# Mixer gates, branches and their sum laid out by tokens instead of by columns, in an encoder kernel on one Trainium2 core

## The chip, the cores and the metric

The kernel runs on one core of one Trainium2 chip. The metric is the device time of one execution in microseconds (us). Before the change it is 1127.99 us, the median of three runs (1127.98 to 1128.56).

## What is computed

Input x is 256 tokens by 1024 channels, in float32. There are two layers; each is a token mixer followed by a feed-forward part (dense in layer 0, eight experts in layer 1). The change is in the mixer, which runs twice:

```python
proj = rms_norm(x) @ w_in + b_in              # 1024 x 6144: q, k, v, u_f, u_x, u_g, gates
y_a = neighbourhood_attention(q, k, v, rpb)   # 8 heads of 64
y_b = fourier_mix(u_f)
y_c = recurrent_branch(u_x, u_g, ...)         # conv, two scans, GeLU gate
y_br = einsum('bskc,kcd->bskd', stack(y_a, y_b, y_c), w_branch)   # 3 x (512 -> 1024)
g = sigmoid(gates).reshape(b, s, 3, 1024)
merged = sum(g * y_br, axis=2)
x = x + merged @ w_out
```

The sigmoid is computed as (1 + tanh(z / 2)) / 2, the factor 1/2 being applied when the sum is split.

## The kernel before

**Weights and units.** All large products run as units. One unit is 512 KB of weights: SyncE loads it into a ring (`raw`, six places), ScalarE rounds it into `w_hi` (L514), VectorE takes the rest into `w_lo` (L900), and TensorE multiplies high by high, high by low and low by high (`mm3`, L1441 to 1445). Rings of four places for `w_hi` and `w_lo` let the splits run three units ahead of TensorE: ScalarE's loop for unit k ends with the high half of unit k+3, which waits until TensorE has done unit k-1; VectorE's loop does likewise.

**A mixer** has 68 units. Units 0 to 47 are twelve groups of four: a group is 512 output columns of `w_in` and 256 rows of it a unit. Their order is u_f, u_x, q, k, v, u_g, and then the six gate groups (units 24 to 47). Units 48 to 59 are the branches, two a product; for each half of the output channels the branches come as Fourier, recurrent, attention. Units 60 to 67 are `w_out`. A group collects in PSUM banks 0 and 1 or 2 and 3, by turns.

**Two orientations.** `unit_columns` (L1452) has the weights stationary and the activations moving: 24 matmuls a unit of 128x256, output with channels on partitions. `unit_tokens` (L1467) has the activations stationary and the weights moving: 12 matmuls a unit of 128x512, output with tokens on partitions. Before, only u_f and v use the second; `w_out` uses its wide relative (L1498).

**Between the units** TensorE does the small products in an order written out by hand: Fourier at units 8 and 12, the recurrent gates at 16 and 25 (L1611), attention at every other unit from 28 (scores L1627, values L1639, transposes L1650). ScalarE and VectorE go through a hand-written list by unit number too. Of the backward scan: at unit 22 ScalarE takes a square root (L676), at 23 VectorE multiplies (L1142), at 24 VectorE takes the second half of u_g (L1042) and runs the forward scan (L1149), and at 25 ScalarE's tanh (L650) waits for that scan and for TensorE's products. These belong to the forward scan up to L1149 and to the backward scan from L650 on.

**Gates, branches, sum.** The gates' bias is one column a channel tile: ScalarE empties a gate group by four tanh of 128x256 with a bias column (L629). A branch product is multiplied by 1 + gate on VectorE (L1182); after the third, two pairs of additions (L1190, L1195) give the sum, ScalarE and VectorE split it straight into `xh` and `xl` (L707, L1202), channels on partitions, as `w_out` needs it.

**GpSimd's queue.** `row` is one tile of 1024 columns in which a vector stands on all 128 partitions; `load_row` (L459) fills it by a DMA. In a mixer it holds the bias of v and u_f, and after VectorE has emptied v (L1029) the next norm's scale is loaded into it.

Of the kernel before, what the change touches and what calls it, by code (L numbers as in the profile page):

```python
# [8 lines left out]
F32 = mybir.dt.float32  # L9
# [8 lines left out]
P = 128  # L18
# [88 lines left out]
def build(nc, x, norm_mix_g, w_in, b_in, rpb, conv_w, conv_b, lru_wa, lru_ba, lru_wx, lru_bx,  # L107
# [12 lines left out]
    with ExitStack() as ctx:  # L120
# [3 lines left out]
        def sem(name):  # L124
# [13 lines left out]
        gates = sb("gates", [P, 3 * KC, SEQ])  # L138
        gflat = gates[:, :, :].rearrange("p c s -> p (c s)")
        hn = gflat[:, 0:TT * D].rearrange("p (t d) -> p t d", t=TT)  # L140
        junk = gflat[:, TT * D:2 * TT * D].rearrange("p (t d) -> p t d", t=TT)
# [55 lines left out]

        O_SP, O_NSP, O_HBA, O_HBX, O_BQ, O_GB = 0, 16, 32, 48, 64, 72
        lam_w = small[:, 96:192].rearrange("p (a b) -> p a b", a=6)
# [50 lines left out]
            sem("s_ps"), sem("s_max"), sem("p_exp"), sem("p_norm"), sem("pt_ps"), sem("pt_ok"), sem("av_ps"), sem("ya_h"), sem("ya_l"))  # L250
        merged, mh_ok, ml_ok = sem("merged"), sem("mh_ok"), sem("ml_ok")

# [16 lines left out]
        ACT_EVACS = [g not in (UF, V) for g in GROUPS] + [False] * len(BRANCHES)  # L269
        DVE_EVACS = [g < GATE0 for g in GROUPS] + [True] * len(BRANCHES)  # L270

        def group_end(l, n):
# [185 lines left out]
        def _(pool):  # L458
# [15 lines left out]
            def mixer(l):  # L474
                load_row(b_in, l * IN_COLS + 2 * BR, normed, 2 * TT * (2 * l + 1))
                for hp in range(HEADS // 2):
                    mask_tables(l, hp)
                load_row(norm_ffn_g, l * D, evac_d, evacs(DVE_EVACS, l, GROUPS.index(V)))

# [18 lines left out]
        def _(act):  # L498
# [69 lines left out]
            def enter(n, B):  # L568
# [10 lines left out]
                for b in range(2):  # L579
                    norm_hi(n, 1, b)  # L580

            def mixer(l):
                B = BASE_MIX[l]
# [16 lines left out]
                for k in range(U_MIX):  # L600
# [9 lines left out]
                    if k <= U_IN and k % 4 == 0 and n >= 0 and ACT_EVACS[n]:  # L610
                        g = GROUPS[n]
                        act.wait_ge(unit_used, group_end(l, n))
                        b0 = 2 * (n % 2)
                        bc = l * NB + 4 * g
                        if g == Q:
                            for m in range(2):
                                i = act.activation(q_t[:, m, :], ps[:, b0, SEQ * m:SEQ * m + SEQ], ACT.Identity,
                                                   scale=SCALE, bias=col2[:, O_BQ + 4 * l + m:O_BQ + 4 * l + m + 1])
                        elif g in (K, UX, UG):
                            for m in range(2):  # L620
                                dst = {K: k_t[:, m, :], UX: ux_t[:, m, 2:2 + SEQ],
                                       UG: ug_t[:, SEQ * m:SEQ * m + SEQ]}[g]
                                i = act.activation(dst, ps[:, b0, SEQ * m:SEQ * m + SEQ], ACT.Identity,
                                                   bias=col[:, bc + m:bc + m + 1])
                        else:

                            for m in range(4):
                                gb = col2[:, O_GB + 24 * l + 4 * (g - GATE0) + m:O_GB + 24 * l + 4 * (g - GATE0) + m + 1]
                                i = act.activation(gates[:, 4 * (g - GATE0) + m, :],  # L629
                                                   ps[:, b0 + m // 2, SEQ * (m % 2):SEQ * (m % 2) + SEQ],  # L630
                                                   ACT.Tanh, scale=0.5, bias=gb)
# [70 lines left out]
                    for dg in range(2):  # L702
                        if k == U_IN + 6 * (dg + 1) + 1:
                            for b in range(2):
                                act.wait_ge(merged, 4 * l + 2 * dg + b + 1)
                                at = 1024 * dg + 512 * b
                                act.activation(xhf[:, at:at + 512], gflat[:, at:at + 512],  # L707
                                               ACT.Copy, scale=0.5).then_inc(mh_ok, 1)
# [177 lines left out]
        def _(dve):  # L886
# [15 lines left out]
            def norm(n, t):  # L902
                dve.wait_ge(rms_ok, TT * n + t + 1)
                link(dve.reciprocal(rinv[:, t:t + 1], rms[:, t:t + 1]))
                if t == 0 and n:
                    dve.wait_ge(row_in, 16 * {1: 2, 2: 3, 3: 5, 4: 6}[n])
                for half in range(2):
# [56 lines left out]
            def set_up_columns():  # L964
# [6 lines left out]
                for l in range(2):  # L971
                    dve.tensor_scalar(col2[:, O_BQ + 4 * l:O_BQ + 4 * l + 4], col[:, l * NB + 4 * Q:l * NB + 4 * Q + 4],
                                      SCALE, None, ALU.mult)
                    dve.tensor_scalar(col2[:, O_GB + 24 * l:O_GB + 24 * l + 24],
                                      col[:, l * NB + 4 * GATE0:l * NB + 4 * GATE0 + 24], 0.5, None, ALU.mult)
                dve.tensor_scalar(lam_w[:, 5, :], col[:, O_LAM:O_LAM + 16], -1.0, 0.0, ALU.mult, ALU.max).then_inc(col_ok, 1)
# [20 lines left out]
            def mixer(l):  # L997
# [15 lines left out]
                for k in range(U_MIX):  # L1013
# [5 lines left out]
                    if k <= U_IN and k % 4 == 0 and n >= 0 and DVE_EVACS[n]:  # L1019
# [4 lines left out]
                        if g in (UF, V):  # L1024
                            dve.wait_ge(row_in, 16 * (3 * l + 1))
                            for t in range(TT):
# [148 lines left out]
                    if U_IN < k <= U_IN + U_BR and (k - U_IN) % 2 == 0:  # L1175
# [3 lines left out]
                        dve.wait_ge(evac_a, evacs(ACT_EVACS, l, n))  # L1179
                        for b in range(2):  # L1180
                            at = br * 2048 + 1024 * dg + 512 * b
                            i = dve.scalar_tensor_tensor(out=gflat[:, at:at + 512], in0=gflat[:, at:at + 512],  # L1182
                                                         scalar=1.0, in1=ps[:, 2 * (n % 2) + b, :],
                                                         op0=ALU.add, op1=ALU.mult)
                        i.then_inc(evac_d, 1)
                        if nb % 3 == 2:
                            dve.wait_ge(evac_d, evacs(DVE_EVACS, l, n))
                            for b in range(2):
                                at = 1024 * dg + 512 * b
                                i = dve.tensor_tensor(gflat[:, 2048 + at:2048 + at + 512], gflat[:, 2048 + at:2048 + at + 512],  # L1190
                                                      gflat[:, 4096 + at:4096 + at + 512], ALU.add)
                            link(i)
                            for b in range(2):
                                at = 1024 * dg + 512 * b
                                dve.tensor_tensor(gflat[:, at:at + 512], gflat[:, at:at + 512],  # L1195
                                                  gflat[:, 2048 + at:2048 + at + 512], ALU.add).then_inc(merged, 1)
                    for dg in range(2):
                        if k == U_IN + 6 * (dg + 1) + 1:
                            for b in range(2):
                                dve.wait_ge(mh_ok, 4 * l + 2 * dg + b + 1)  # L1200
                                at = 1024 * dg + 512 * b
                                dve.scalar_tensor_tensor(out=xlf[:, at:at + 512], in0=gflat[:, at:at + 512], scalar=0.5,  # L1202
                                                         in1=xhf[:, at:at + 512].bitcast(F32), op0=ALU.mult,
                                                         op1=ALU.subtract).then_inc(ml_ok, 1)
# [233 lines left out]
        def _(pe):  # L1438
# [27 lines left out]

            def unit_tokens(base, k, r, banks, i=0, per=0):  # L1467

                wh, wl = split(base, k, i, per)
                for kk in range(2):  # L1470
                    for t in range(TT):
                        c = 2 * r + kk
                        ins = mm3(ps[:, banks + t, :], xh[:, c, P * t:P * t + P], xl[:, c, P * t:P * t + P],
                                  wh[:, 512 * kk:512 * kk + 512], wl[:, 512 * kk:512 * kk + 512],
                                  first=(c == 0), last=(c == KC - 1))
                ins.then_inc(unit_used, 1)

            def unit_tokens_tile(base, k, r, bank, t):
# [74 lines left out]
            def mixer(l):  # L1553
# [11 lines left out]
                for k in range(4, U_MIX - 4):  # L1565
# [86 lines left out]
                    if k < U_IN:  # L1652
# [6 lines left out]
                        if GROUPS[n] in (UF, V):  # L1659
                            unit_tokens(B, k, r, 2 * (n % 2))  # L1660
                        else:
                            unit_columns(B, k, r, 2 * (n % 2), (xhf, xlf), SEQ, last=KC - 1)
                    elif k < U_IN + U_BR:
# [10 lines left out]
                        unit_columns(B, k, r, 2 * (n % 2), (yhf[:, 1024 * br:1024 * br + 1024], ylf[:, 1024 * br:1024 * br + 1024]),  # L1674
                                     SEQ, last=BC - 1)
# [261 lines left out]
```

## Time and profile before

| what | value |
|---|---|
| median of three runs | 1127.99 us |
| profiled execution | 1127.95 us |
| its span, first to last instruction | 1126.1 us |
| mean granted TensorE clock | 0.992 |
| TensorE busy | 1105.6 us (98%) |
| VectorE busy | 871.0 us (77%) |
| ScalarE busy | 720.6 us (64%) |
| mixer of layer 0, first unit to last | about 10 to 234 us |
| mixer of layer 1 | about 440 to 664 us |

The busy times are sums over the whole span. The records of neighbouring matmuls overlap, so the time that a matmul takes from the next one is the distance between their starts, not its length.

### The profile page before, as it was taken

To read this page: it belongs to the slowest core of one execution; us is meant where nothing else is said; L and a number is where in the kernel's file an instruction comes from. 1 tells how busy PE (TensorE), PEld (TensorE's weight loads), DVE (VectorE), ACT (ScalarE), POOL (GpSimd) and SP (SyncE) were. 2 spreads that over 40 slices of the span, in tenths; PEclk is the share of its full clock that TensorE was granted. 3 is DMA by queue.
4 is the path that set the end of the run, shared out by engine and by line. 5 is a ranking of instruction groups with operands and counts; after the bars stand their busy time and mean duration, and the time that the engine had idled before them with its cause. 6 is when DMAs were issued, how large, how long until landed. Compare 5 with 4: busy or idle time off the path is not lost.

```text
span 1126.1 us, 19254 instructions
## 1 busy us (share of the span) xinstructions
PE 1105.6 (98%) x6858; PEld 970.8 (86%) x6858; DVE 871.0 (77%) x1064; ACT 720.6 (64%) x978; POOL 53.7 (5%) x29
## 2 busy tenths in 40 slices
PE   7999999999999999999999999999999999999996
PEld 6989999989999998989989988878888888888884
DVE  6975885864554457766885868999999999999996
ACT  6376664464444446356665457888888888887884
POOL 0300000000000000200000000101010101101010
PEclk9999999999999999999999998999999999999998
DMA  9955445565555657755445469999999999999951
GB/s 307 248 167 156 141 146 186 179 194 184 186 174 161 222 186 211 207 160 176 134 140 182 159 229 399 371 379 347 362 362 354 382 336 391 339 389 334 389 210 40
DMA packets 139500, 276.47 MB, mean 246 GB/s; under 512 B 26608, under 2 KB 26928, under 8 KB 139440
## 3 DMA queue, kind: packets, MB, share of 16 engines
q1 hardware_dynamic: 136976, 267.20, 70.1%
q0 software_dynamic: 2304, 8.39, 2.0%
q8 instruction: 39, 0.64, 0.2%
q14 instruction: 21, 0.17, 0.0%
q10 hardware_dynamic: 160, 0.07, 0.0%
HBM read 273.52 MB, written 2.10 MB: 245 GB/s over the span
## 4 chain that ended last, share of the span: by engine, by line
PE 88%; DVE 6%; ACT 4%; issue 1%; DMA 0%; DVEq 0%; ACTq 0%
PE ps L1443 27%; PE ps L1445 27%; PE ps L1444 27%; PE ps L1611 1%; DVE w_lo L900 1%; ACT w_hi L514 1%; PE ps L1764 1%; PE ps L1835 1%; PE ps L1639 1%; DVE yl L900 1%; PE ps L1585 1%; ACT p_t L695 1%; PE ps L1750 1%; PE ps L1650 1%; PE ps L1529 1%
## 5 line engine op out<-in xcount | busy, mean ns | idle before, releaser
L900 DVE TENSOR_TENSOR w_lo<-raw,w_hi 128x1024 fp32r<-128x1024 f32 x268 | 326.1, 1233 | 154.3 <-ACT w_hi L514 152.1
L514 ACT ACTIVATE w_hi<-raw 128x1024 fp32r<-128x1024 f32 x268 | 281.4, 1059 | 180.3 <-PE ps L1445 177.6
L1443 PE MATMUL ps<-xh,w_hi 128*128 128x256 f32 x960 | 274.5, 286 | 0.0
L1444 PE MATMUL ps<-xl,w_hi 128*128 128x256 f32 x960 | 271.6, 283 | 0.0
L1445 PE MATMUL ps<-xh,w_lo 128*128 128x256 f32 x960 | 271.6, 283 | 0.0
L1443 PEld LDWEIGHTS ps<-xh,w_hi 128*128 128x128 f32 x960 | 184.1, 192 | 2.6 <-issue 2.1
L1444 PEld LDWEIGHTS ps<-xl,w_hi 128*128 128x128 f32 x960 | 184.1, 192 | 0.4
L1445 PEld LDWEIGHTS ps<-xh,w_lo 128*128 128x128 f32 x960 | 184.0, 192 | 0.0
L1443 PE MATMUL ps<-w_hi,xh 128*128 128x512 f32 x432 | 172.0, 398 | 1.1 <-DVE xl L927 0.8
L1444 PE MATMUL ps<-w_lo,xh 128*128 128x512 f32 x432 | 169.2, 392 | 0.0
L1445 PE MATMUL ps<-w_hi,xl 128*128 128x512 f32 x432 | 169.1, 392 | 0.0
L900 DVE TENSOR_TENSOR w_lo<-mix,w_hi 128x1024 fp32r<-128x1024 f32 x128 | 152.6, 1219 | 11.0 <-ACT w_hi L514 8.7
L514 ACT ACTIVATE w_hi<-mix 128x1024 fp32r<-128x1024 f32 x128 | 134.4, 1060 | 32.8 <-PE ps L1445 32.7
L1443 PEld LDWEIGHTS ps<-w_hi,xh 128*128 128x128 f32 x432 | 81.8, 189 | 22.3 <-DVE w_lo L900 2.6
L1445 PEld LDWEIGHTS ps<-w_hi,xl 128*128 128x128 f32 x432 | 81.7, 189 | 17.5
L1444 PEld LDWEIGHTS ps<-w_lo,xh 128*128 128x128 f32 x432 | 81.7, 189 | 16.1
L900 DVE TENSOR_TENSOR yl<-mix,yh 128x1024 fp32r<-128x1024 f32 x64 | 77.1, 1218 | 0.7
L514 ACT ACTIVATE yh<-mix 128x1024 fp32r<-128x1024 f32 x64 | 67.8, 1062 | 15.2 <-PE ps L1445 15.2
L1443 PE MATMUL ps<-w_hi,yh 128*128 128x512 f32 x192 | 76.6, 399 | 0.7
L1445 PE MATMUL ps<-w_hi,yl 128*128 128x512 f32 x192 | 75.0, 390 | 0.0
L1444 PE MATMUL ps<-w_lo,yh 128*128 128x512 f32 x192 | 74.9, 390 | 0.0
L1443 PE MATMUL ps<-yh,w_hi 128*128 128x256 f32 x192 | 54.5, 284 | 0.0
(229 smaller groups left out, 1591.1 us busy)
## 6 DMA issues: line engine op xcount, KB each, us to landing
mix<-in_moe_w_gu_dram SPq DMA_DIRECT2D x112, 512.0 KB, 7.6
raw<-in_w_in_dram SPq DMA_DIRECT2D x96, 512.0 KB, 4.3
raw<-in_moe_w_gu_dram SPq DMA_DIRECT2D x80, 512.0 KB, 5.8
mix<-in_moe_w_down_dram SPq DMA_DIRECT2D x80, 512.0 KB, 5.5
raw<-in_ffn_w_gu_dram SPq DMA_DIRECT2D x48, 512.0 KB, 4.0
raw<-in_w_branch_dram SPq DMA_DIRECT2D x24, 512.0 KB, 3.6
raw<-in_ffn_w_down_dram SPq DMA_DIRECT2D x24, 512.0 KB, 4.7
raw<-in_w_out_dram SPq DMA_DIRECT2D x16, 512.0 KB, 3.5
```

Of the source, the lines that this page charges most:

```text
L514: act.activation(halves(u)[0], src, ACT.Copy).then_inc(hi_done, 1)
L695: ins = act.activation(p_t[:, j % 2, hh, :], p_t[:, j % 2, hh, :], ACT.Exp, bias=nmax[:, j % 2, hh:hh + 1], accum_out=rsum[:, j % 2, hh:hh ...
L900: dve.tensor_tensor(w_l, place(u)[0], w_h.bitcast(F32), ALU.subtract).then_inc(lo_done, 1)
L1443: mm(dst, ah, bh, start=first, stop=False, skip_group_check=True)
L1444: mm(dst, ah, bl, start=False, stop=False, skip_group_check=True)
L1445: return mm(dst, al, bh, start=False, stop=last, skip_group_check=True)
L1529: ins = pe.transpose(dst, hn[:, t, P * (4 * b + c):P * (4 * b + c) + P], ident)
L1585: ins = mm(ps[:, 4 + m, 0:SEQ], uf_t[:, BR * t + P * m:BR * t + P * m + P], cst[:, at:at + SEQ], start=(t == 0), stop=(t == TT - 1))
L1611: ins = mm(ps[q, 4 + 2 * g + m // 2, SEQ * (m % 2):SEQ * (m % 2) + SEQ], wlru[q, d, g, m, :], conv_t[q, m, :], start=True, stop=True)
L1639: ins = mm(ps[HD * hh:HD * hh + HD, 6, P * t:P * t + P], v_t[:, kt, HD * hd:HD * hd + HD], pt_t[:, hh, P * kt:P * kt + P], start=(kt == 0) ...
L1650: ins = pe.transpose(ps[:, 7, at:at + P], p_t[:, j % 2, hh, P * kt:P * kt + P], ident)
L1750: ins = pe.transpose(ps[:, 6 + c // 4, P * (c % 4):P * (c % 4) + P], xrow[:, P * c:P * c + P], ident)
```

## The change

Gate groups and branch products go from `unit_columns` to `unit_tokens`. The gate bias can then no longer be a column of ScalarE's tanh; it is copied as rows into the PSUM banks before the group (`seed`), and the group's first matmul adds to it. `row` gets three more loads a mixer. The sum comes out with tokens on partitions, and TensorE turns it by transposes (`turn_merged`).

```diff
+                for j in range(3):          # GpSimd, after v is emptied
+                    if j:
+                        load_row(b_in, l * IN_COLS + BR * GATE0 + D * j, seeded, 6 * l + 2 * j)
+                    else:
+                        load_row(b_in, l * IN_COLS + BR * GATE0, evac_d, evacs(DVE_EVACS, l, GROUPS.index(V)))
+                load_row(norm_ffn_g, l * D, seeded, 6 * l + 6)
...
+            def seed(l, j):                 # ScalarE
+                n = len(GROUPS) - 6 + j
+                act.wait_ge(row_in, 16 * (6 * l + 2 + j // 2))
+                act.wait_ge(evac_a, evacs(ACT_EVACS, l, n - 2))
+                act.wait_ge(evac_d, evacs(DVE_EVACS, l, n - 2))
+                for t in range(TT):
+                    ins = act.activation(ps[:, 2 * (n % 2) + t, :], row[:, BR * (j % 2):BR * (j % 2) + BR], ACT.Copy)
+                ins.then_inc(seeded, 1)
...
-                            for m in range(4):
-                                i = act.activation(gates[...], ps[:, b0 + m // 2, ...], ACT.Tanh, scale=0.5, bias=gb)
+                            for t in range(TT):
+                                i = act.activation(by_token[:, t, gate_columns(g)], ps[:, b0 + t, :], ACT.Tanh, scale=0.5)
+                    if 22 <= k < U_IN - 4 and k % 4 == 2:
+                        seed(l, (k - 22) // 4)
...
-                        if k == U_IN + 6 * (dg + 1) + 1:
+                        if k == U_IN + 6 * (dg + 1) + (3, 2)[dg]:     # ScalarE; VectorE alike
+                            for t in range(TT):
+                                act.wait_ge(mt_ps, TT * (2 * l + dg) + t + 1)
+                                act.activation(xh[...], ps[:, (4, 0)[dg] + t, :]..., ACT.Copy, scale=0.5)
...
+            def turn_merged(l, dg):         # TensorE
+                pe.wait_ge(merged, 2 * l + dg + 1)
+                for t in range(TT):
+                    for c in range(4):
+                        at = 512 * dg + P * c
+                        ins = pe.transpose(ps[:, (4, 0)[dg] + t, P * c:P * c + P], by_token[:, t, at:at + P], ident)
+                    ins.then_inc(mt_ps, 1)
...
+                        elif GROUPS[n] >= GATE0:
+                            if r == 0:
+                                pe.wait_ge(seeded, 6 * l + n - len(GROUPS) + 7)
+                            unit_tokens(B, k, r, 2 * (n % 2), seed=True)
...
+                        if k == U_IN + 8:
+                            turn_merged(l, 0)
+                        unit_tokens(B, k, r, 2 * (n % 2), ah=yh, al=yl, c0=BC * br, last=BC - 1)
...
-                        if r % 2 == 0:
-                            pe.wait_ge(ml_ok, 4 * l + r // 2 + 1)
+                        if r == 0:
+                            pe.wait_ge(ml_ok, 4 * l + 2)
+                        if r == 2:
+                            turn_merged(l, 1)
```

On VectorE the products and sums keep their number and size (128x512) and address token rows; the sum of the second and third branch's products is taken one branch earlier. The bias columns halved for the tanh are no longer set up. The waits that count `row` loads get the new numbers.

## Rows read from the trace of the kernel before

**Rows 1.** The page: busy time of the engines, and engines on the chain.

```profile
PE 1105.6 (98%) x6858; PEld 970.8 (86%) x6858; DVE 871.0 (77%) x1064; ACT 720.6 (64%) x978; POOL 53.7 (5%) x29
...
PE 88%; DVE 6%; ACT 4%; issue 1%; DMA 0%; DVEq 0%; ACTq 0%
```

**Rows 2.** The chain of waits around the attention of layer 0 (start, us, what).

```profile
104.96 0.66 PE ps L1627 x4
...
140.94 0.44 DVE yl L1120
...
141.51 0.51 PE ps L1639 x5
```

**Rows 3.** Busy time by stretch: first unit 28 to 38, then the branches.

```profile
104.90:141.50 36.60, 35.93 (x293) 32.88 (x293) 30.43 (x48) 26.60 (x53) 0.00 (x0) 1.00 0.45 136
177.40:212.50 35.10, 35.10 (x296) 34.93 (x296) 24.71 (x29) 15.60 (x19) 0.00 (x0) 1.00 0.55 179
```

**Rows 4.** Timeline of TensorE, units 16 to 20 (start, us, line, shape).

```profile
67.31 0.40 PE L1444 MATMUL ps<-w_lo,xh 128*128 128x512 f32 x1
...
77.76 0.39 PE L1445 MATMUL ps<-w_hi,xl 128*128 128x512 f32 x1
77.99 0.28 PE L1443 MATMUL ps<-xh,w_hi 128*128 128x256 f32 x1
...
80.86 0.28 PE L1443 MATMUL ps<-xh,w_hi 128*128 128x256 f32 x1
```

**Rows 5.** Timeline of TensorE, eight transposes between matmuls of the dense part.

```profile
264.57 1.04 PE L1694 MATMUL ps<-cst,gates 128*128 128x128 f32 x8
...
265.56 0.28 PE L1444 MATMUL ps<-xl,w_hi 128*128 128x256 f32 x1
```

**Rows 6.** Loads of the row tile: start in layer 0, issues with us to landing.

```profile
80.07 0.58 POOL L463 DMA_DIRECT2D row<-in_norm_ffn_g_dram  x1 [29.85 <-DVE mix L1029]
...
row<-in_norm_ffn_g_dram POOLq DMA_DIRECT2D x1, 512.0 KB, 6.6
...
row<-in_norm_ffn_g_dram POOLq DMA_DIRECT2D x1, 512.0 KB, 7.3
...
DMA to landing us min/median/max: 5.2/6.6/7.3
```

**Rows 7.** Timeline of ScalarE, units 22 to 25; idle time before in brackets.

```profile
82.20 1.28 ACT L676 ACT_TABLE_LOAD   x1
...
92.85 1.28 ACT L650 ACT_TABLE_LOAD   x1 [1.37 <-DVE mix L1149]
96.19 1.57 ACT L650 ACTIVATE mix<-ps,col 128x256 f32<-128x256 f32 x4 [2.05 <-PE ps L1611]
```

**Rows 8.** Timeline of VectorE, units 22 to 28.

```profile
85.53 1.22 DVE L900 TENSOR_TENSOR w_lo<-raw,w_hi 128x1024 fp32r<-128x1024 f32 x1 [1.10 <-ACT w_hi L514]
...
89.70 0.88 DVE L1042 TENSOR_SCALAR mix<-ps,col 128x256 f32<-128x256 f32 x2 [0.39 <-PE ps L1445]
90.49 2.28 DVE L1149 TENSOR_TENSOR_SCAN mix<-mix 128x1024 f32<-128x1024 f32 x1
...
105.64 0.69 DVE L1105 TENSOR_TENSOR p_t<-ps,mix 128x512 f32<-128x512 f32 x1 [0.38 <-PE ps L1627]
```

**Rows 9.** Timeline of ScalarE at unit 32: a gate group emptied, and a 128x512 copy.

```profile
121.74 1.57 ACT L629 ACTIVATE gates<-ps,col 128x256 f32<-128x256 f32 x4
123.18 0.61 ACT L690 ACTIVATE pt_t<-ps 128x512 f32<-128x512 f32 x1
123.66 0.53 ACT L695 ACTIVATE p_t<-p_t,small 128x256 f32<-128x256 f32 x1
```

**Rows 10.** Timelines of VectorE and TensorE at unit 42.

```profile
155.86 0.42 DVE L1120 TENSOR_TENSOR yl<-ps,yh 128x256 fp32r<-128x256 f32 x1 [0.71 <-ACT yh L701]
...
156.62 0.66 PE L1639 MATMUL ps<-pt_t,mix 128*64 128x128 f32 x8
```

**Rows 11.** Timeline of VectorE at unit 60: the last product, before the sum.

```profile
212.84 1.28 DVE L1182 SCALAR_TENSOR_TENSOR gates<-gates,ps 128x512 f32<-128x512 f32 x2 [0.50 <-PE ps L1445]
```

More of the change, by code:

```diff
@@ L139, in build @@
         gflat = gates[:, :, :].rearrange("p c s -> p (c s)")
+        by_token = gflat.rearrange("p (t n) -> p t n", t=TT)
         hn = gflat[:, 0:TT * D].rearrange("p (t d) -> p t d", t=TT)
@@ L196, in build @@
         N_COL = O_LAM + 4 * BC
-        O_SP, O_NSP, O_HBA, O_HBX, O_BQ, O_GB = 0, 16, 32, 48, 64, 72
+        O_SP, O_NSP, O_HBA, O_HBX, O_BQ = 0, 16, 32, 48, 64
         lam_w = small[:, 96:192].rearrange("p (a b) -> p a b", a=6)
@@ L250, in build @@
             sem("s_ps"), sem("s_max"), sem("p_exp"), sem("p_norm"), sem("pt_ps"), sem("pt_ok"), sem("av_ps"), sem("ya_h"), sem("ya_l"))
-        merged, mh_ok, ml_ok = sem("merged"), sem("mh_ok"), sem("ml_ok")
+        seeded, merged, mt_ps, mh_ok, ml_ok = sem("seeded"), sem("merged"), sem("mt_ps"), sem("mh_ok"), sem("ml_ok")
         ft_ps = sem("ft_ps")
@@ L270, in build, with gate_columns @@
         DVE_EVACS = [g < GATE0 for g in GROUPS] + [True] * len(BRANCHES)
+        def gate_columns(g):
+            return slice(512 * (g - GATE0), 512 * (g - GATE0) + 512)
         def group_end(l, n):
@@ L625, in mixer @@
                         else:
-                            for m in range(4):
[L628 to L631, printed above, removed]
+                            for t in range(TT):
+                                i = act.activation(by_token[:, t, gate_columns(g)], ps[:, b0 + t, :], ACT.Tanh, scale=0.5)
                         i.then_inc(evac_a, 1)
+                    if 22 <= k < U_IN - 4 and k % 4 == 2:
+                        seed(l, (k - 22) // 4)
                     if k == AT_F1:
@@ L702, in mixer @@
                     for dg in range(2):
-                        if k == U_IN + 6 * (dg + 1) + 1:
[L704 to L707, printed above, removed]
+                        if k == U_IN + 6 * (dg + 1) + (3, 2)[dg]:
+                            for t in range(TT):
+                                act.wait_ge(mt_ps, TT * (2 * l + dg) + t + 1)
+                                act.activation(xh[:, 4 * dg:4 * dg + 4, P * t:P * t + P],
+                                               ps[:, (4, 0)[dg] + t, :].rearrange("p (c s) -> p c s", c=4),
                                                ACT.Copy, scale=0.5).then_inc(mh_ok, 1)
@@ L905, in norm @@
                 if t == 0 and n:
-                    dve.wait_ge(row_in, 16 * {1: 2, 2: 3, 3: 5, 4: 6}[n])
+                    dve.wait_ge(row_in, 16 * {1: 5, 2: 6, 3: 11, 4: 12}[n])
                 for half in range(2):
@@ L1024, in mixer @@
                         if g in (UF, V):
-                            dve.wait_ge(row_in, 16 * (3 * l + 1))
+                            dve.wait_ge(row_in, 16 * (6 * l + 1))
                             for t in range(TT):
@@ L1179, in mixer @@
                         dve.wait_ge(evac_a, evacs(ACT_EVACS, l, n))
[L1180 to L1183, printed above, removed]
+                        a, b, c = (slice(D * i + 512 * dg, D * i + 512 * dg + 512) for i in range(3))
+                        q = (a, b, c)[br]
+                        for t in range(TT):
+                            i = dve.scalar_tensor_tensor(out=by_token[:, t, q], in0=by_token[:, t, q],
+                                                         scalar=1.0, in1=ps[:, 2 * (n % 2) + t, :],
                                                          op0=ALU.add, op1=ALU.mult)
@@ L1187, in mixer @@
                             dve.wait_ge(evac_d, evacs(DVE_EVACS, l, n))
[L1188 to L1191, printed above, removed]
+                            for t in range(TT):
+                                i = dve.tensor_tensor(by_token[:, t, a], by_token[:, t, a], by_token[:, t, b], ALU.add)
@@ L1192, in mixer @@
+                            i.then_inc(merged, 1)
+                        elif nb % 3 == 1:
+                            dve.wait_ge(evac_d, evacs(DVE_EVACS, l, n))
+                            for t in range(TT):
+                                i = dve.tensor_tensor(by_token[:, t, b], by_token[:, t, b], by_token[:, t, c], ALU.add)
                             link(i)
[L1193 to L1196, printed above, removed]
@@ L1197, in mixer @@
                     for dg in range(2):
[L1198 to L1203, printed above, removed]
+                        if k == U_IN + 6 * (dg + 1) + (3, 2)[dg]:
+                            for t in range(TT):
+                                at = (slice(None), slice(4 * dg, 4 * dg + 4), slice(P * t, P * t + P))
+                                dve.wait_ge(mh_ok, TT * (2 * l + dg) + t + 1)
+                                dve.scalar_tensor_tensor(out=xl[at], in0=ps[:, (4, 0)[dg] + t, :].rearrange("p (c s) -> p c s", c=4),
+                                                         scalar=0.5, in1=xh[at].bitcast(F32), op0=ALU.mult,
@@ L1465, in unit_columns, with unit_tokens @@
                 return ins
-            def unit_tokens(base, k, r, banks, i=0, per=0):
+            def unit_tokens(base, k, r, banks, i=0, per=0, ah=xh, al=xl, c0=0, last=KC - 1, seed=False):
                 wh, wl = split(base, k, i, per)
@@ L1472, in unit_tokens @@
                         c = 2 * r + kk
-                        ins = mm3(ps[:, banks + t, :], xh[:, c, P * t:P * t + P], xl[:, c, P * t:P * t + P],
+                        ins = mm3(ps[:, banks + t, :], ah[:, c0 + c, P * t:P * t + P], al[:, c0 + c, P * t:P * t + P],
                                   wh[:, 512 * kk:512 * kk + 512], wl[:, 512 * kk:512 * kk + 512],
-                                  first=(c == 0), last=(c == KC - 1))
+                                  first=(c == 0 and not seed), last=(c == last))
                 ins.then_inc(unit_used, 1)
+            def turn_merged(l, dg):
+                pe.wait_ge(merged, 2 * l + dg + 1)
+                for t in range(TT):
+                    for c in range(4):
+                        at = 512 * dg + P * c
+                        ins = pe.transpose(ps[:, (4, 0)[dg] + t, P * c:P * c + P], by_token[:, t, at:at + P], ident)
+                    ins.then_inc(mt_ps, 1)
             def unit_tokens_tile(base, k, r, bank, t):
@@ L1673, in mixer @@
                                 pe.wait_ge(y_ok, count)
-                        unit_columns(B, k, r, 2 * (n % 2), (yhf[:, 1024 * br:1024 * br + 1024], ylf[:, 1024 * br:1024 * br + 1024]),
-                                     SEQ, last=BC - 1)
+                        if k == U_IN + 8:
+                            turn_merged(l, 0)
+                        unit_tokens(B, k, r, 2 * (n % 2), ah=yh, al=yl, c0=BC * br, last=BC - 1)
                     else:
                         r = k - U_IN - U_BR
-                        if r % 2 == 0:
-                            pe.wait_ge(ml_ok, 4 * l + r // 2 + 1)
+                        if r == 0:
+                            pe.wait_ge(ml_ok, 4 * l + 2)
+                        if r == 2:
+                            turn_merged(l, 1)
                         unit_wide(B, k, xh[:, r, :], xl[:, r, :], TT, r == 0, False)
```

3 lines of the change are left out of this document (removed).

## The prediction, made before the changed kernel was run

> **What bounds the kernel now.** I read the page first: TensorE is busy 98% of the span and holds 88% of the chain that ended last [rows 1]. That says TensorE, but the chain has a second part. Asked in order of time, it leaves TensorE at 104.96 us, at unit 28 where attention begins, and comes back only at 141.51 at unit 38; between the two it runs through ScalarE and VectorE alone [rows 2]. In the same stretch TensorE is busy 35.93 of 36.60 us [rows 3]: the two other engines deliver just in time, and TensorE waits once, about 0.7 us. Layer 1 has the same rows. So a mixer has three kinds of place: before unit 28 and after unit 42 a shorter TensorE unit is a shorter run, and in the branches TensorE is busy 35.10 of 35.10 us [rows 3]; between 28 and 42 it is the list of ScalarE and VectorE that counts, and TensorE saves nothing there.
>
> **A unit on TensorE.** Starts, not lengths, give the price. From 67.31 to 77.76 us there are 46 steps of 128x512: 10.45 / 46 = 0.227 us. From 77.99 to 80.86 there are 24 steps of 128x256: 0.120 us [rows 4]. A unit by columns is 24 x 0.120 = 2.88 us, one by tokens 12 x 0.227 = 2.73 us: 0.153 us less (with 0.12 and 0.19 as ends, by the rounding of the starts). 36 units a mixer change: 24 of gates, 12 of branches.
>
> **Turning the sum.** It is new: eight transposes twice a mixer. In the dense part eight of them stand between matmuls: from the first of them to the second matmul behind them 0.99 us, less one step of 0.12, is 0.87 us [rows 5]. Four turns cost 3.5 us (upper end 4.2, by their recorded 1.04 us). Their waits should be free: at unit 60 VectorE starts the product 0.5 us into its turn, two of it take 1.28 us [rows 11], and the one pair of additions left behind it I take as long; 2.6 us, against 5.4 us until TensorE turns at unit 62. After that the copy and the split of two 128x512 tiles, about 2 us, have two units again before the second half of `w_out`. The turn at unit 56 has the same 5.4 us, and its split three units. If one such cover were gone, a turn would show at most some 2 us more.
>
> **ScalarE's list.** Emptying a gate group is four tanh of 128x256, started 1.44 us apart from what follows (121.74 to 123.18); a 128x512 instruction goes in 0.48 us (123.18 to 123.66) [rows 9]. So the tanh become 0.96, a gain of 0.48, and the seed adds two copies, 0.96 us. A copy from `row` into PSUM is not in the trace: between 0.36 (the 128x256 step) and 0.61 us (the recorded length); I take 0.48, the nearest in shape. Six times a mixer ScalarE has 0.48 us more. Seeds 2 to 5 (units 30, 34, 38, 42) fall where it waits for VectorE several us anyway. They delay only things that have slack.
>
> **The first seed, which decides.** It stands at unit 22, ahead of the square root, in a queue that runs in order. Its bias row is asked for when v is emptied: in the trace GpSimd issues the load of the same tile at the same place at 80.07 us, and it takes 6.6 us to land in layer 0 and 7.3 in layer 1, where the shortest load of this tile took 5.2 [rows 6]. Nothing before unit 20 changes, so I take these two numbers. ScalarE reaches the seed at about 82.20 [rows 7] and stands until 86.67; the two copies end at 87.65. Behind it wait the square root, the high halves of units 25 and 26, and the first half of u_g. TensorE does not yet suffer: it has its units up to 24, and the small products at 25 give it 3.6 us. VectorE does. Its low half of unit 25 comes 5.4 us late, then the product, the low half of 26, u_g and the forward scan run without the 0.4 us pause that they have now [rows 8]. ScalarE's table load and tanh at unit 25 wait for that scan. Now the load comes at 92.85 and ScalarE then waits 2.05 us for TensorE before the tanh [rows 7]. The delay is thus 5.4 - 0.4 - 2.0 = 3.0 us in layer 0 and 3.7 in layer 1. In general it is the landing time less 3.6 us; below 3.6 us it is nothing.
>
> From there it goes 1:1 into the attention. The second seed (unit 26) adds 0.96 us; VectorE's pause of 0.38 before the first scores' sum is used up [rows 8], which makes 3.6; the tanh at unit 32, which are on the chain [rows 2, 9], give back 0.48. So the list is 3.1 us late at unit 38 (layer 0) and 3.8 (layer 1). TensorE, which would be 0.6 us early at unit 28, catches up with the list and waits there by bits, at units 32, 34, 36 and 38, for VectorE's maxima and the split of the attention output. The last such place is unit 42: the split at 155.86 takes 0.42 us, TensorE starts 0.15 us behind such a split, hence at 156.43 + 3.1 = 159.5 in place of 156.62 [rows 10]: +2.9, and +3.6 in layer 1.
>
> **The sum.** From unit 42 to 47 six units give back 0.9 us: +2.0 and +2.7. The branches give 24 x 0.153 = 3.7 us back over both layers, the turns take 3.5. Together 2.0 + 2.7 - 3.7 + 3.5 = +4.5 us. The profiled execution had 1127.95 us (span 1126.1), which is the median of the runs to 0.04; so 1132.4 us.
>
> The later row loads cost nothing: the second is asked for after seed 1, near 102 us, and needed at unit 30, near 115; the third after seed 3, with four units again. GpSimd waits in between with nothing else queued. TensorE's own wait for the first seed is covered: copied by 87.7, needed at 89.6.
>
> **A rule that speaks otherwise.** Rows 6 have 6.6 and 7.3 us. The Trainium skill, page DMA: Bandwidth & Descriptors, section Anatomy of one DMA, gives for transfers issued from GpSimd about 2.0 us plus bytes over 436 GB/s, an estimate of 3.2 us for these 512 KB. By it the row would be there before the 3.6 us from which the delay counts, and the time would be that of rival 1. The trace disagrees by twice, on this very queue and tile.
>
> **Rivals.**
> 1. *The first seed's wait hides* (faster): the row lands within 3.6 us of its issue, or ScalarE and VectorE take up the delay. For it: GpSimd's queue is idle before it, and ScalarE has pauses of 1 to 2 us at each unit there. Against it: rows 6, and that VectorE is nearly solid from unit 25 to 28's start. Then the list is 0.96 - 0.38 - 0.48 = +0.1 late, TensorE at unit 42 -0.1, at 48 -1.0 a mixer: -2.0 - 3.7 + 3.5 = -2.2: 1125.7 us. Chance 0.20.
> 2. *TensorE alone counts* (faster): all 72 units give 0.153 us, less the turns: -11.0 + 3.5 = -7.5: 1120.4 us. Rows 1 speak for it, rows 2 against. Chance 0.05.
> 3. *Half of the delay is absorbed* (no change): the load lands in its shortest time, 5.2 us, in both layers, so that the delay is 1.6 instead of 3.0 and 3.7: 4.5 - 3.5 = +1.0: 1129.0 us. Chance 0.15.
> 4. *A turn waits as well* (slower by more): with VectorE behind, the sum is late for unit 56 or 62, up to 2 us for each of four turns, beside +4.5: some 1136. Rows 11 leave 2.8 us for it. Chance 0.08.
>
> The forecast has 0.52. What is below 0.2% (2.3 us) this kernel's measurement can't tell from no change, so the bounds are 1125.7 and 1130.3. Slower: forecast 0.50, rival 4, a part of 3: 0.60. Same: most of 3, half of 1 (which lies on the bound): 0.22. Faster: 0.18. The range is 1125.3 to 1134.6: at the lower end rival 1, at the upper the forecast with landings a us longer in both layers; the forecast's own range is 1130 to 1134.
>
> **What the profile after would show.** Steps of 0.227 us in gate and branch units. ScalarE idle 4 to 5 us ahead of the first seed, ended by the DMA of `row`; the forward scan ending near 97.8 instead of 92.8 us; the first scores' sum on VectorE near 109 instead of 105.64; TensorE waiting at units 32 to 38 for VectorE; the values product of unit 42 near 159.5. No wait ahead of the transposes. I am wrong if the first seed does not wait, or if the scan's delay meets a pause on ScalarE or VectorE that I have counted as work.

## The result, and the profile after

| | before | after | predicted |
|---|---|---|---|
| median | 1127.99 us | 1135.42 us (5 runs, 1133.58 to 1137.5) | 1132.4 (1125.3 to 1134.6) |
| ratio | | 1.006, 95% interval 1.0049 to 1.0071 | 1.0039 |
| profiled execution, its span | 1127.95, 1126.1 | 1135.58, 1133.4 | |
| end of mixer 0 / mixer 1 (first turn of the norm) | 233.62 / 663.80 us | 236.73 / 669.68 us | +1.9 / +4.5 |
| from there to the end of the span | 462.3 us | 463.7 us | 0 |

The changed kernel is slower, as forecast and for the reason forecast, but by 7.4 us in place of 4.5, and the time lies 0.8 us above the range. Of the 7.3 us between the two spans, 3.1 arise in mixer 0, 2.8 in mixer 1 (all of it behind its unit 20, where the changed kernel is still 3.1 us late), and 1.4 behind both mixers, where the change has no instruction. The last term was not in the prediction. Another 0.3 us lies outside the span: the device time is 2.2 us longer than the span in the changed kernel and 1.9 us in the kernel before. The two medians are 1.0066 apart, in the upper part of the interval; beside the experiments below, the kernel before had medians of 1128.7 to 1128.9 us and the changed kernel once 1135.08, which is 6.4 us in place of 7.4.

First the page of the changed kernel, against [rows 1]. TensorE has less work (832 fewer matmul records) and holds 10 points less of the chain; what it lost went to VectorE, ScalarE, issue and DMA. An engine that was made cheaper and holds less of the chain points to a new wait.

```profile
PE 1102.6 (97%) x6026; PEld 927.6 (82%) x6026; DVE 868.0 (77%) x1062; ACT 725.6 (64%) x978; POOL 56.6 (5%) x35
...
PE 78%; DVE 8%; ACT 8%; issue 3%; DMA 2%; SPq 0%; DVEq 0%; ACTq 0%
```

The chain of waits around unit 22 of layer 0 (start, us, what) names it. Before, the chain was TensorE's until 104.96 [rows 2]; now it leaves at v's emptying and goes through the load of the bias row.

```profile
78.66 1.29 DVE mix L1045 x2
80.25 7.34 DMA row<-in_b_in_dram
88.75 1.28 ACT L694
...
91.01 1.05 ACT w_hi L524
...
93.37 1.24 DVE mix L1158
94.64 1.23 DVE w_lo L918
95.86 0.79 DVE mix L1058 x2
96.64 2.21 DVE mix L1165
98.92 1.28 ACT L668
```

ScalarE's timeline, against [rows 7] (start, us, line; idle time before in brackets): the seed stands 5.25 us for the row, and the table load at unit 25 then waits for the scan. The tanh starts at 100.22 instead of 96.19.

```profile
87.61 1.12 ACT L599 ACTIVATE ps<-row 128x512 f32<-128x512 f32 x2 [5.25 <-DMA row<-in_b_in_dram]
88.75 1.28 ACT L694 ACT_TABLE_LOAD   x1
...
98.92 1.28 ACT L668 ACT_TABLE_LOAD   x1 [4.26 <-DVE mix L1165]
100.22 1.57 ACT L668 ACTIVATE mix<-ps,col 128x256 f32<-128x256 f32 x4
```

VectorE's timeline, against [rows 8]: it idles 7.48 us for ScalarE's high half of unit 25, the scan starts at 96.56 instead of 90.49, the first scores' sum at 110.25 instead of 105.64.

```profile
92.08 1.22 DVE L918 TENSOR_TENSOR w_lo<-raw,w_hi 128x1024 fp32r<-128x1024 f32 x1 [7.48 <-ACT w_hi L524]
...
96.56 2.28 DVE L1165 TENSOR_TENSOR_SCAN mix<-mix 128x1024 f32<-128x1024 f32 x1
...
110.25 0.68 DVE L1121 TENSOR_TENSOR p_t<-ps,mix 128x512 f32<-128x512 f32 x1
```

TensorE's timeline: it waits for VectorE at units 32, 34, 36, 38 and 42. The values product of unit 38 stands at 145.70 (141.51 in [rows 2]), that of 42 at 160.61 (156.62 in [rows 10]).

```profile
119.69 0.70 PE L1652 MATMUL ps<-mix 64*128 64x256 f32 x4 [1.34 <-DVE small L1124]
...
127.87 0.70 PE L1652 MATMUL ps<-mix 64*128 64x256 f32 x4 [0.93 <-DVE small L1124]
...
136.12 0.70 PE L1652 MATMUL ps<-mix 64*128 64x256 f32 x4 [0.88 <-DVE small L1124]
...
145.70 0.66 PE L1664 MATMUL ps<-pt_t,mix 128*64 128x128 f32 x8 [1.24 <-DVE yl L1136]
...
160.61 0.66 PE L1664 MATMUL ps<-pt_t,mix 128*64 128x128 f32 x8 [0.27 <-DVE yl L1136]
```

Busy time by stretch, against [rows 3]: TensorE is busy 35.42 of 40.80 us in the attention where it was 35.93 of 36.60, and still 35.10 of 35.10 in the branches.

```profile
104.90:145.70 40.80, 35.42 (x173) 25.86 (x173) 32.44 (x49) 31.21 (x58) 0.53 (x1) 1.00 0.51 167
180.50:215.60 35.10, 35.10 (x165) 28.98 (x165) 26.87 (x32) 15.41 (x18) 0.00 (x0) 1.00 0.54 179
```

### The profile page after: what moved, and what is told of

Its sections match the earlier page's. It is cut to its first block, busy times and chain, and to the rows that moved or that the text cites. A ratio compares the mean times of both kernels' runs of the same rounds, so it can differ in the third digit from the quotient of the medians.

```text
span 1133.4 us, 17620 instructions
## 1 busy us (share of the span) xinstructions
PE 1102.6 (97%) x6026; PEld 927.6 (82%) x6026; DVE 868.0 (77%) x1062; ACT 725.6 (64%) x978; POOL 56.6 (5%) x35
## 4 chain that ended last, share of the span: by engine, by line
PE 78%; DVE 8%; ACT 8%; issue 3%; DMA 2%; SPq 0%; DVEq 0%; ACTq 0%
PE ps L1459 24%; PE ps L1461 24%; PE ps L1460 24%; ACT w_hi L524 2%; DVE w_lo L918 2%; DMA row<-in_b_in_dram 1%; PE ps L1796 1%; PE ps L1867 1%; ACT mix L668 1%; ACT p_t L713 1%; DVE small L1123 1%; DVE p_t L1121 1%; ACT mix L678 1%; PE ps L1636 1%; DMA raw<-in_w_in_dram 1%
## 5 line engine op out<-in xcount | busy, mean ns | idle before, releaser
L1459 PE MATMUL ps<-w_hi,xh 128*128 128x512 f32 x624 | 249.8, 400 | 1.3 <-DVE xl L945 0.8
L1460 PE MATMUL ps<-w_lo,xh 128*128 128x512 f32 x624 | 244.3, 392 | 0.0
L1461 PE MATMUL ps<-w_hi,xl 128*128 128x512 f32 x624 | 244.3, 391 | 0.0
L1459 PE MATMUL ps<-xh,w_hi 128*128 128x256 f32 x576 | 164.0, 285 | 0.0
L1460 PE MATMUL ps<-xl,w_hi 128*128 128x256 f32 x576 | 163.0, 283 | 0.0
L1461 PE MATMUL ps<-xh,w_lo 128*128 128x256 f32 x576 | 162.9, 283 | 0.0
L1459 PEld LDWEIGHTS ps<-xh,w_hi 128*128 128x128 f32 x576 | 110.5, 192 | 0.5
L1460 PEld LDWEIGHTS ps<-xl,w_hi 128*128 128x128 f32 x576 | 110.5, 192 | 0.4
L1461 PEld LDWEIGHTS ps<-xh,w_lo 128*128 128x128 f32 x576 | 110.5, 192 | 0.0
L1459 PEld LDWEIGHTS ps<-w_hi,yh 128*128 128x128 f32 x288 | 54.1, 188 | 14.9 <-issue 3.9
```

What stands on the lines that cost most here:

```text
L1459: mm(dst, ah, bh, start=first, stop=False, skip_group_check=True)
L1460: mm(dst, ah, bl, start=False, stop=False, skip_group_check=True)
L1461: return mm(dst, al, bh, start=False, stop=last, skip_group_check=True)
```

## The experiments

Each comes with runs of the kernel before on the same chip; ratios are to those.

**Seed 0 moved to where ScalarE idles** (end of unit 23, behind the high half of unit 26), all else as changed.

```diff
-                    if 22 <= k < U_IN - 4 and k % 4 == 2:
+                    if 26 <= k < U_IN - 4 and k % 4 == 2:
                         seed(l, (k - 22) // 4)
...
+                    if k == 23:
+                        seed(l, 0)
```

> The changed kernel with the first seed alone moved, from the start of unit 22 on ScalarE's list to the end of unit 23. All loads, copies, units and turns stay. Theory (the first seed's wait for its row stands ahead of the square root and delays the list of ScalarE and VectorE by some 4 us a mixer): the wait is then after the high half of unit 26, near 88 us, when the row has just landed; the list is on time, TensorE is level at unit 42 and about 1 us ahead at unit 48, and the time is 1125 to 1127.5 us. Rival (the three added loads, or ScalarE's added copies, cost the time, wherever the first wait stands): 1133 us or more, since none of them is taken away. Rival (the matmuls by tokens or the turns are dearer than I counted): 1130 or more.

Measured 1127.88 us, ratio 0.9989 (0.998 to 0.9999), 0.4 us above the range of the theory. ScalarE's timeline:

```profile
88.14 1.10 ACT L599 ACTIVATE ps<-row 128x512 f32<-128x512 f32 x2
...
96.35 1.57 ACT L668 ACTIVATE mix<-ps,col 128x256 f32<-128x256 f32 x4 [1.92 <-PE ps L1638]
```

The seed starts half a microsecond later than in the changed kernel, yet nothing waits: the row is there, and ahead of the tanh 1.92 us of waiting for TensorE are back. So it is not the seed's work but what stands behind it in the queue while it waits. The first scores' sum is at 106.38, +0.74 to before (0.6 forecast for the second seed's copies), and mixer 1 ends at 661.92, 1.9 us earlier than before (rival 1 had 2.2). Behind the mixers 2.4 us more pass than before; see below.

**Seeds 0 and 1 both in idle places** (ends of units 23 and 24).

```diff
-                    if 22 <= k < U_IN - 4 and k % 4 == 2:
+                    if 30 <= k < U_IN - 4 and k % 4 == 2:
                         seed(l, (k - 22) // 4)
...
+                    if k in (23, 24):
+                        seed(l, k - 23)
```

> The changed kernel with the first seed at the end of unit 23 and the second at the end of unit 24 of ScalarE's list, where it waits for the scan and for TensorE; before, the second stood between the two tanh of the backward scan. Theory: as the run with the first seed moved, and 0.96 us less on the list between units 25 and 28 in each mixer, of which TensorE can use what it is ahead: 0.5 to 1 us a mixer less than that run, 1124 to 1126 us. Rival (the list has slack again once the first wait is gone): the same as that run to 0.3 us.

Measured 1125.97 us, ratio 0.998 (0.9971 to 0.9989). The first scores' sum is at 105.35, mixer 1 ends at 659.95: 3.9 us earlier than before. With both seeds out of the way the shorter units show.

**Each turn done twice.**

```diff
-                    for c in range(4):
+                    for c in (0, 1, 2, 3, 0, 1, 2, 3):
```

> The changed kernel with every transpose of the sum done twice (16 instead of 8 a turn). Theory: a turn stands bare on TensorE; the matmuls around the second eight are 0.8 us further apart, 4 x 0.8 = 3.3 us on the changed kernel's time, some 1138.7 us. Rival (the turns fill time in which TensorE would wait anyway): the changed kernel's 1135.4 us.

Measured 1139.15 us, ratio 1.0096 (1.008 to 1.0111). TensorE's timeline at unit 56, first as changed, then doubled:

```profile
203.12 1.03 PE L1500 MATMUL ps<-cst,gates 128*128 128x128 f32 x8
203.91 0.48 PE L1459 MATMUL ps<-w_hi,yh 128*128 128x512 f32 x1
```

```profile
202.56 1.91 PE L1500 MATMUL ps<-cst,gates 128*128 128x128 f32 x16
204.22 0.48 PE L1459 MATMUL ps<-w_hi,yh 128*128 128x512 f32 x1
```

From the transposes to the next matmul 0.79 us became 1.66: eight more cost 0.87 us, the price in the prediction, and four times that is 3.5 us, as forecast. The medians are 3.7 us apart from the changed kernel on another chip. No wait stands ahead of any turn in the changed kernel's timeline, so rival 4 falls.

**The seeds alone, in the kernel before**: three bias loads and six seeds as in the change, no new orientation. The seeded bias is then overwritten by the group's first matmul, and the tanh keep their columns.

```diff
+                    if 22 <= k < U_IN - 4 and k % 4 == 2:
+                        seed(l, (k - 22) // 4)
...
+                            if n >= 6:
+                                pe.wait_ge(seeded, 6 * l + n - 5)
```

> The kernel before with the row loads, the six seeds a mixer at their places in the change, and TensorE's wait for them, but gates, branches and sum as before: the first matmul of a gate group overwrites the seeded rows and the tanh keeps its bias column. Theory: the wait alone delays the list as in the changed kernel, 0.5 us more because the tanh stay four of 128x256, and no shorter units give any of it back: +4 to +4.8 us a mixer, 1136 to 1137.6 us. Rival (the time lies in the products by tokens or in the turns, which are not in this kernel): 1128 to 1129.5 us.

Measured 1137.59 us, ratio 1.0082 (1.0067 to 1.0098). The whole loss is in the seeds, and the rest of the change seems to give 0.0022 of it back, 2.5 us; the intervals of the two ratios overlap, but mixer 1 of the profiled executions ends at 671.84 us here and at 669.68 in the changed kernel, 2.2 us apart.

**The changed kernel again**, on the chip of the next two.

> The changed kernel once more, beside the two below on one chip. Theory: its wait for the first row is there in every execution, so all of them lie 5 us or more above the kernel before; what varies between them (1133.6 to 1137.5 in the first five) is the time at half clock at the routing, so a lower mean clock goes with a longer run, by about 0.5 us for each us at half clock. Rival (the spread comes from the landing of the row): no relation to the clock. 1134 to 1137.5 us.

Measured 1135.08 us, ratio 1.0057 (1.0044 to 1.007). In its profile the row comes 0.5 us earlier in layer 0 (seed at 87.09), and everything behind it too. In layer 1 it lands in 6.6 us, and mixer 1 ends at 668.46: 4.7 us behind the kernel before, where the first profile had 5.9. The expectation tied the spread between executions to the clock alone; five runs don't show that: the two with a mean clock of 0.992 have spans of 1131.2 and 1132.9 us.

**The first half of the row early**: its 512 columns are loaded when u_f is emptied, into the half that the bias of v does not need.

```diff
+                load_half(BR, l * IN_COLS + BR * GATE0, evac_d, evacs(DVE_EVACS, l, 0), half_in)
...
+                if j == 0:
+                    act.wait_ge(half_in, 16 * (l + 1))
```

> The changed kernel with all seeds at their places, but the first gate group's 512 bias columns are loaded right after u_f is emptied (unit 4), into the half of the row that u_f has freed; the second group's 512 columns come after v, as before. Theory (what costs is that the row is not there when ScalarE comes to it, not where the seed stands): as the run with the first seed moved, since two copies ahead of the square root, 0.96 us, are less than the 2.05 us that ScalarE waits for TensorE at unit 25: list on time, 1126 to 1129 us. Rival (the place ahead of the square root is dear by itself): 1130 us or more.

Measured 1127.11 us, ratio 0.9988 (0.9979 to 0.9996). ScalarE's timeline:

```profile
82.34 1.10 ACT L606 ACTIVATE ps<-row 128x512 f32<-128x512 f32 x2
```

The seeds keep their places and the first starts without a wait; the scores' sum is at 106.35, as with the moved seed. Two ways to take away the wait agree to 0.03 us here and to 0.0001 in the ratio (the medians, on two chips, are 0.8 us apart).

**The first half alone**: the load after v is cut in two of 256 KB, and seed 0 waits for the first only.

```diff
+                for j in range(2):
+                    load_half(BR * j, ..., evac_d, evacs(DVE_EVACS, l, GROUPS.index(V)), (half_in, row_in)[j])
```

> The changed kernel with the first row load of the gates cut into two halves of 256 KB, both asked for when v is emptied, and the first seed waiting for the first half alone. Theory (the delay is the landing time less 3.6 us, one to one): the first half lands about 5 to 6 us after its issue instead of 7.3, so the list is 1.3 to 2.3 us less late in each mixer: 1131 to 1133.5 us, and the tanh at unit 25 starts earlier than in the changed kernel by what the seed starts earlier. Rival (above some threshold the delay is absorbed or jumps): the unit 38 and 42 waits don't follow the seed's start one to one. If half a load lands as late as a whole one, the time is the changed kernel's.

Measured 1132.38 us, ratio 1.0035 (1.0023 to 1.0048). ScalarE's timeline:

```profile
86.42 1.12 ACT L606 ACTIVATE ps<-row 128x512 f32<-128x512 f32 x2 [4.37 <-DMA row<-in_b_in_dram]
```

The half that the seed waits for still needs 6.5 and 6.0 us to land in the two layers, and the half behind it 6.9 and 6.5 (5.5 in the run before this one, where a half travels alone at this place). Halving the bytes does not halve the landing time.

These runs give the relation that the prediction rested on (us in the profile):

| layer 0 | seed starts | first scores' sum | values product, unit 38 |
|---|---|---|---|
| changed | 87.61 | 110.25 | 145.70 |
| changed, again | 87.09 | 109.73 | 145.17 |
| turns doubled | 87.07 | 109.70 | 145.14 |
| seeds in the kernel before | 86.85 | 109.48 | 145.34 |
| changed + filler (below) | 86.72 | 109.36 | 144.80 |
| first half alone | 86.42 | 109.05 | 144.50 |
| first half early | 82.34 | 106.35 | 141.80 |
| seed 0 moved | 88.14, no wait, not ahead of the list | 106.38 | 141.83 |

Wherever the seed waits at unit 22, the scores' sum comes 22.64 us behind it, to 0.01 us, in layer 1 as well (521.03 to 543.66, 518.62 to 541.26). Without a wait it comes at 106.36. Unit 38 follows 35.45 us behind the scores' sum; in the seeds-alone run it is 35.86, since there the tanh of unit 32 give nothing back (0.48 in the prediction). The wait thus costs from a seed start of 106.36 - 22.64 = 83.7 us on: 3.6 us after an issue near 80.1, the threshold of the prediction. No run has a seed that starts between 82.34 and 86.42, so the corner itself is extrapolated from both sides.

**The stretch behind the mixers.** What was left is 1.4 us where nothing changed. The granted clock by stretch shows it; first the kernel before, then the changed one (times of the second are 6 us later for the same work; TensorE, its weight loads, VectorE, ScalarE, GpSimd, then TensorE's granted clock).

```profile
670.00:682.00 12.00, 11.46 (x79) 10.61 (x78) 8.21 (x26) 6.13 (x9) 1.58 (x3) 0.81 1.04 396
682.00:690.00 8.00, 8.00 (x27) 6.55 (x27) 6.03 (x16) 4.84 (x7) 0.00 (x0) 0.64 1.04 406
```

```profile
682.00:690.00 8.00, 8.00 (x39) 7.90 (x39) 3.54 (x10) 3.50 (x6) 0.00 (x0) 0.50 1.04 406
690.00:698.00 8.00, 8.00 (x26) 6.34 (x25) 6.76 (x17) 4.94 (x7) 0.00 (x0) 0.68 1.04 401
```

At the routing of the experts TensorE drops to its lower level, 1.2 GHz, behind short products between which it waits for VectorE (11.46 of 12.00 us busy). Over windows of 3 to 5 us, twice the missing clock times the length adds up to 10.3 us there before, with both seeds moved, in the seeds-alone run and with the early half, 13.6 to 13.7 us in the changed kernel, its repetition, the doubled turns, seed 0 moved and the first half alone. The rest of the span behind mixer 1 is 462.3 to 462.9 us in the first group and 463.5 to 464.7 in the second. The code there is the same, and the change is not needed for the longer one: the kernel before seems to have both. Of its 62 runs beside the experiments, 27 have a mean clock of 0.992, as its profile, and spans of 1126.6 us on average, and 21 have 0.990, as the changed kernel's profile, and 1127.6 us. What decides between the two lengths stays open. That the stretch costs time was tested by filling TensorE's waits with more of the filler transposes that stand there (`route`).

```diff
-                keep_warm(3)
+                keep_warm(8)
                 positions(0)
-                keep_warm(4)
+                keep_warm(10)
...
-                keep_warm(3)
+                keep_warm(8)
```

*With both seeds moved:*

> The changed kernel with seeds 0 and 1 at the ends of units 23 and 24, and more filler transposes at the routing in layer 1 (26 in place of 10, in three places where TensorE waits for VectorE). The question is the stretch at half clock behind mixer 1, which was 10.2 us long in the kernel before and in the run with seeds 0 and 1 moved, and 13.6 us in the changed kernel. Theory 1: the short pauses of TensorE at the routing let the clock fall; with more work in them the half-clock stretch in the first 40 us behind mixer 1 shrinks below 6 us, and by 0.49 us per us at half clock the run is 2 us shorter than its sibling without the filler (1125.97 us), less up to 1.4 us for filler that ends behind what it was to cover: 1124 to 1125.5 us. Theory 2: the pauses are not what decides; the stretch stays at 10.2 or 13.6 us and the filler costs 0 to 1.4 us: 1126 to 1129 us.

*In the kernel before:*

> The kernel before with the same extra filler transposes at the routing, as in the run beside it. Theory 1: half-clock stretch behind mixer 1 below 6 us, 1126 to 1127.6 us (ratio below 1). Theory 2: stretch unchanged at 10.2 or 13.6 us, 1128 to 1130 us (ratio 1.000 to 1.0015).

*In the changed kernel:*

> The changed kernel as it is, with the extra filler at the routing, so that the change can be read against the kernel before with the same filler (1126.77 us, ratio 0.998) without the half-clock stretch, which was 13.6 us long here and 10.3 us there. Theory 1: of the +7.4 us of the change, about 1.3 us are that difference in the stretch, by chance of its length and not by work; without it the change costs what the two mixers show, 2.9 + 2.8 = 5.7 and the +0.2 of the start: about 1126.8 + 6.0 = 1132.8 us, ratio near 1.0035. Theory 2: the longer stretch was not the cause, or the filler doesn't remove it here; then the difference between the two stays at +7 or more: 1134 us or more.

Measured: 1122.83 us, ratio 0.9947 (0.9934 to 0.9961), 1.2 us below what the first theory gave (it took the stretch of the unfilled run as 10.3 us, while 8 of that run's 11 executions have a mean clock of 0.990 or less; that this is the reason is not tested); 1126.77 us, ratio 0.998 (0.9971 to 0.9989); 1132.23 us, ratio 1.0032 (1.002 to 1.0044). Windows of the kernel before with filler:

```profile
670.00:682.00 12.00, 11.74 (x103) 11.21 (x102) 8.89 (x28) 7.45 (x11) 1.58 (x3) 1.00 1.04 396
682.00:690.00 8.00, 6.63 (x30) 5.14 (x28) 6.76 (x17) 4.94 (x7) 0.00 (x0) 1.00 1.04 408
```

The clock stays at its upper level, 2.4 GHz, here in all three kernels. Ahead of it TensorE is busy 11.74 us of 12.00 in place of 11.46, and behind it has pauses again, 6.63 of 8.00 us busy, where before it worked through all 8.00 at the lower level. From the end of mixer 1 to the end of the span it is now 461.1, 461.0 and 461.1 us in the three, against 462.4 with the seeds moved, 462.3 before, 463.7 changed. So the 1.4 us were the stretch. Changed against before, both with filler, the ratios are 0.0052 apart, 5.9 us (by their intervals some 1.7 more or less); that is the change without the stretch.

The kernel with seeds 0 and 1 in idle places and the filler, at 1122.83 us, beats both: 0.53% below the kernel before. Its profile has another stretch at the lower level, of about 3 us, in the attention of layer 0:

```profile
138.00:141.00 3.00, 1.48 (x14) 0.74 (x12) 2.22 (x7) 2.37 (x7) 0.00 (x0) 1.00 0.56 179
141.00:144.50 3.50, 3.50 (x16) 2.75 (x13) 3.43 (x4) 2.40 (x4) 0.00 (x0) 0.58 0.21 27
```

Two of its five runs have a mean clock of 0.995, as this profile, and are the two longest of the five, 1123.91 and 1124.3 us.

## Why the prediction was right, and where not

- *What bounds where.* Right. TensorE gains in the branches only what the turns take (from unit 48 to the end of mixer 0: 55.63 us before, 55.55 after), and nothing in the attention.
- *A unit by tokens.* -0.153 us each was near (the rows unrounded, 2.87 less 2.73 us, give 0.144): from the values product of unit 42 to unit 48 it is 21.37 us before and 20.57 after, 0.80 for six units instead of 0.92.
- *Turns.* Right: 0.87 us each, no wait. The 2.6 us that VectorE was to need ahead of a turn left out the 0.5 us at which it starts; the margin was then 2.3 us, and the profile has 2.6 (additions done at 217.7, turn at 220.33).
- *The first seed decides.* Right: the two runs without the wait are at 0.9989 and 0.9988, and the lines of the runs with and without a wait meet at 3.6 us.
- *Size of the wait in layer 0.* Too small. I took 6.6 us for the landing [rows 6], it took 7.34; by the 1:1 rule that is 0.7 us. In layer 1 7.3 was taken and 7.21 came. Over the ten profiles in which the whole 512 KB are loaded at this place, they took 6.1 to 7.3 us in layer 0 and 6.6 to 7.7 in layer 1, so one landing out of one profile was worth a range of a microsecond a layer. Hence the mixers' loss is not one number either: 5.9 us in the first profile, 4.7 in the repetition and 4.7 with filler (against the same profile of before). That 4.5 was forecast for it is right within this spread, and the first profile lies at its upper end.
- *From the seed to unit 42.* Another 0.3 us in layer 0: the row was issued at 80.25 instead of 80.07, and the seed's two copies held ScalarE 1.14 us (87.61 to 88.75) where 0.96 was taken. Unit 42 came at 160.61 against 159.5 forecast (+0.7 of landing makes 160.2).
- *The sum.* 4.5 forecast; the mixers gave 5.9, which is 1.4 more: 0.7 the landing (-0.1 in layer 1), 0.2 the later issue, 0.2 to 0.3 the six units of both layers, and some 0.3 the first seed's copies, which take 1.14 us in layer 1 too. With these alone the time would lie inside the range.
- *The step that failed* is one I did not write: that everything behind mixer 1 takes the time it took. The sum ends with mixer 1 (2.0 + 2.7 - 3.7 + 3.5) and puts the rest at nothing without a reason. It took 1.4 us more: TensorE ran at its lower level for 13.6 us there in place of 10.3, and 0.3 us more lie outside the span. The trace of before had the stretch, in the clock column of its windows (0.81 and 0.64 above), but I had read the windows of the mixers alone [rows 3], where it is 1.00. With its two lengths in the sum the upper end would have been near 1136 us. Part of the miss is luck: the before profile, to which the sum was added, has the shorter stretch, and the kernel before has medians 0.7 to 0.9 us above 1127.99 in all later groups of runs.
- *Rivals.* Rival 1 described the two runs without the wait: 1125.7 forecast, 1127.88 and 1127.11 measured, mixers right to 0.3 us. Rivals 2 and 4 found no support; a landing of 5.2 us, rival 3, did not occur at this place for 512 KB (shortest 6.1).

## What to carry to other kernels

An instruction that waits for a transfer costs what is queued behind it, not what it does: put it where its engine idles anyway, or ask for the data earlier. Before pricing an edit, find for each wait the latest time that costs nothing (here some 3.6 us after the issue), and take the transfer's duration as a spread and not as a number. And read the granted clock over the whole span: a stretch at the lower level that short pauses bring on belongs in the range even of an edit made elsewhere, and filling such pauses was worth 0.2% by itself here.

## What the runs showed that I had not expected

- The landing of a broadcast row by GpSimd depends more on where the load stands than on its size: 512 KB took 6.1 to 7.7 us at the deciding place (twenty readings) and 5.3 us in the median of the eight bias loads of the changed kernel; 256 KB took 6.0 to 6.9 us there with two in flight, 5.5 us alone there, and 6.6 and 5.9 us behind u_f. The Trainium skill, page DMA: Bandwidth & Descriptors, section Anatomy of one DMA, gives 2.0 us plus bytes over 436 GB/s, an estimate of 3.2 and 2.6 us. The trace disagrees by 3 to 4.5 us at the deciding place; whether the 0.6 us between the two sizes is right these runs can't tell, since the spread at one size is larger.
- The half-clock stretch at the routing has one of two lengths, 10.3 or 13.6 us, in nine profiles of one stretch of code, and 16 more small transposes take it away (three profiles of three).
